# A hybrid decoder step on one core: from one shared front and a 160/384 split to two halves of 256 and 288 columns

## The reference, cut to what matters

```
proj = rmsnorm(x) @ w_in                    # 31 blocks of 128 features (lru, gate, q latent, kv latent, rope key, memory q)
y_lru = rglru(causal_conv(xr)) * gelu(gr)   # a recurrence along the tokens
o_mla = latent attention, 16 heads, causal  # the prompt against itself; the samples also against 2048 cached tokens
o_mem = attention into 256 memory tokens    # the samples against their own cached keys and values
merged = g_l*(y_lru@w_o_lru) + g_a*(o_mla@w_o_mla) + g_m*(o_mem@w_o_mem)
x = x + merged @ w_out
```

```
q = h @ w_peer_query; s = q . sub_keys      # 16 score vectors of 128
top 16 of each, top 16 of the 16x16 sums    # per head: 8 heads x 16 = 128 experts per token
act = gelu(peer_u[idx] . h)                 # 128 rows of 2048 numbers gathered from peer_u
x = x + sum((w * act) * peer_v[idx])        # 128 rows of 2048 numbers gathered from peer_v
y = rmsnorm(x)
```

## Time and profile before

| what | value |
|---|---|
| median of 3 runs | 4582.04 us (4579.02 to 4588.62) |
| span of the profiled execution | 4584.9 us, 2.9 us above the median |
| PE busy | 3686.9 us, 80% |
| DVE busy | 2780.3 us, 61% |
| ACT busy | 391.7 us, 9% |
| POOL busy | 1501.0 us, 33% |
| DMA | 1413.36 MB, mean 308 GB/s |

### The profile page before, as it was taken

One profiled execution on the slowest core, in us unless ns is written; L12 is line 12 of the kernel. 1 busy time (PEld: TensorE's weight loads), 2 busy tenths in 40 slices (PEclk: granted clock), 3 DMA queues, 4 the chain that ended last, 5 costly groups with the idle time before them and its releaser, 6 DMA issues.

```text
span 4584.9 us, 37965 instructions
## 1 busy us (share of the span) xinstructions
PE 3686.9 (80%) x13918; PEld 2304.1 (50%) x13918; DVE 2780.3 (61%) x3641; ACT 391.7 (9%) x882; POOL 1501.0 (33%) x1217
## 2 busy tenths in 40 slices
PE   8999999988999999999999999999999980000000
PEld 6888846653999575555555456444444430000000
DVE  3224324431000167887777568888965569899998
ACT  1012122321000100000000010000000000000000
POOL 0000100024000013454454445444332227777763
PEclk9999999998999999999999999999999995555555
DMA  4121261137666678998999989999999999999998
GB/s 168 65 74 65 101 235 44 42 126 268 239 241 242 231 290 325 395 388 358 422 421 403 375 356 387 404 403 401 394 412 396 423 423 409 398 409 410 411 412 367
DMA packets 223666, 1413.36 MB, mean 308 GB/s; under 512 B 33312, under 2 KB 42400, under 8 KB 59488
## 3 DMA queue, kind: packets, MB, share of 16 engines
q0 software_dynamic: 137424, 904.11, 48.5%
q1 hardware_dynamic: 72768, 471.37, 27.0%
q10 hardware_dynamic: 13296, 35.52, 2.0%
HBM read 1385.11 MB, written 25.75 MB: 308 GB/s over the span
## 4 chain that ended last, share of the span: by engine, by line
PE 71%; DMA 13%; POOL 5%; issue 5%; DVE 4%; ACT 1%; SPq 0%; ACTq 0%; DVEq 0%; POOLq 0%
PE psum L975 26%; PE psum L1116 13%; PE psum L627 12%; DMA arena<-in_v,arena 12%; PE psum L1095 4%; POOL arena L582 3%; DVE psum L2062 3%; POOL arena L602 2%; PE psum L1080 2%; PE psum L1043 1%; PE psum L1023 1%; PE psum L699 1%; PE psum L709 1%; PE psum L869 1%; PE psum L868 1%
## 5 line engine op out<-in xcount | busy, mean ns | idle before, releaser
L975 PE MATMUL psum<-arena 128*128 128x160 f32 (+1 forms) x5120 | 1176.1, 393 | 0.8 <-DVE arena L1746 0.8
L975 PEld LDWEIGHTS psum<-arena 128*128 128x128 f32 x5120 | 836.2, 190 | 340.1 <-DVE arena L1746 0.9
L2062 DVE SCALAR_TENSOR_TENSOR psum<-arena,psum 128x2048 f32<-128x2048 f32 x381 | 897.1, 2355 | 165.1 <-DMA arena<-in_v,arena 155.3
L582 POOL DMA_INDIRECT arena<-in_v,arena x544 | 651.5, 1198 | 742.5 <-DVE psum L2062 325.7
L582 POOL DMA_INDIRECT arena<-in_u,arena x288 | 484.5, 1682 | 1222.2 <-DVE arena L1853 513.4
L1116 PE MATMUL psum<-arena 128*128 128x512 f32 x2048 | 882.2, 594 | 0.6 <-ACT arena L1433 0.6
L1116 PEld LDWEIGHTS psum<-arena 128*128 128x128 f32 x2048 | 390.1, 191 | 492.1 <-issue 492.1
L627 PE MATMUL psum<-arena 128*128 128x272 f32 x2432 | 562.0, 392 | 0.9 <-issue 0.9
L627 PEld LDWEIGHTS psum<-arena 128*128 128x128 f32 x2432 | 460.8, 190 | 98.8 <-issue 5.5
L1940 DVE SCALAR_TENSOR_TENSOR arena<-arena,pages 128x2048 f32<-128x2048 f32 x128 | 300.9, 2351 | 72.6 <-DMA arena<-in_v,arena 67.6
L1897 DVE CUSTOM_DVE_ANT_0 arena<-arena 128x2048 f32<-128x2048 f32 x128 | 287.6, 2288 | 58.7 <-DMA arena<-in_u,arena 57.9
(11 more groups left out here) (298 smaller groups left out, 2675.7 us busy)
## 6 DMA issues: line engine op xcount, KB each, us to landing
arena<-in_w_merge SPq DMA_DIRECT2D x160, 1024.0 KB, 5.6
arena<-in_u_cols SPq DMA_DIRECT2D x128, 1024.0 KB, 9.4
arena<-in_w_out SPq DMA_DIRECT2D x32, 1024.0 KB, 4.9
arena<-in_w_query SPq DMA_DIRECT2D x32, 1024.0 KB, 7.8
arena<-in_w_proj SPq DMA_DIRECT2D x31, 1024.0 KB, 4.8
products<-arena ACTq DMA_DIRECT2D x32, 512.0 KB, 13.8
arena<-in_pool_keys SPq DMA_DIRECT2D x64, 192.0 KB, 4.1
arena<-in_v,arena POOLq DMA_INDIRECT x544, 12.0
```

The source lines that it names most:

```text
L582: pool.indirect_dma_start(row, None, A[table], bass.IndirectOffsetOnAxis(ap=idx[:, r:r + 1], axis=0))\
L975: last = mm(out, w[:, (off + k) * P:(off + k + 1) * P], src[:, k0 + k, lo:hi], start=(k == 0), stop=(k == n - 1))
L2062: V.scalar_tensor_tensor(a, four(row), atmp_b[:, t, r:r + 1], a if r else four(x1_b[:, t, :]), ALU.mult, ALU.add).then_inc(s("rows_used"), 1)
```

## The change

The prompt is cut in two halves, and every stage is run for half A (tiles 0 and 1, 256 columns), then for half B (tiles 2 and 3 and the samples, 288 columns). Memory keys and values are computed once, in A. The projection and latent weights, once streamed for 544 columns, are now streamed twice (31 + 16 DMAs more); the merge, out and query weights were streamed twice already. All weights use one ring of 3 slots (the early stages had 5). The page keys of the samples have 4 slots (5 before).

The rows come in the order `JOBS` = u 0, u 1, v 0, v 1, u 4, v 4, v 2, v 3: tiles 0 and 1 are gathered in full, while half B runs; dense is for tiles 2 and 3. Again 832 rows: 288 u and 544 v. DVE takes them so: 10 during `query_a`, 10 in B's convolutions, 12 in B's recurrence, 8 in B's memory attention, 40 in B's latent attention (80 up to there), none in the attention of the samples, 160 in B's merge, 28 in its out, 4 after it, 40 in its query (312), then 264 beside dense, and 256 in the last loop. The `pairs` of tiles 0 and 1 stand in B's convolutions and recurrence too.

```diff
-A_TILES, B_TILES = (3, 4), (0, 1, 2)
-JOBS = (("u", 3), ("u", 4), ("v", 3), ("v", 4), ("u", 2), ("v", 2), ("v", 0), ("v", 1))
-HELD = 88
+HA = Half("a", 0, HALF, (0, 1), False)
+HB = Half("b", HALF, HALF + SAMP, (2, 3), True)
+JOBS = (("u", 0), ("u", 1), ("v", 0), ("v", 1), ("u", 4), ("v", 4), ("v", 2), ("v", 3))
+FEWER, MORE, MOST = 4, 5, 6
+EARLY_ROWS = 80
...
+STAGES = (("proj_a", NPROJ), ("mem_k", 8), ("mem_v", 8), ("mla_a", 16), ("merge_a", 80), ("out_a", 16), ("query_a", 16),
+          ("proj_b", NPROJ), ("cache", 2 * NB), ("mla_b", 16), ("mla_v", 2), ("merge_b", 80), ("out_b", 16), ("query_b", 16), ("dense", U_TILES))
...
                     c = first_row[table, t] + r
+                    if c == C4:
+                        sample_pages()
...
-                    if (table, t, r) == ("v", 2, HELD):
+                    if (table, t, r) == ("v", 2, MOST - 1):
                         pool.wait_ge(s("products_stored0"), 256)
                         pool.wait_ge(s("products_stored1"), 256)
-                    if table == "v" and t in (2, 0, 1):
-                        if t == 2:
-                            upto = max(0, AHEAD * (r + 1 - HELD) // (n - HELD))
-                        else:
-                            upto = min(AHEAD + P * t + r + 1, DENSE * P)
+                    if table == "v" and t in (2, 3):
+                        upto = min(AHEAD + P * (t - 2) + r + 1, DENSE * P) if t > 2 or r >= MOST - 1 else 0
                         for e in range(asked, upto):
...
+            pe.wait_ge(s("x_normed"), since("x_normed", HB) + KD)
+            projections(HB)
+            memory_attention(HB)
+            latent_attention(HB)
+            sample_attention(HB)
+            merges(HB)
+            output(HB)
+            expert_query(HB)
...
+            for c in range(8):
+                conv(HB, c)
+                if c % 2 == 1 and c < 6:
+                    pairs(0, c + 1)
+                else:
+                    take(2)
+            for c in range(8):
+                if c == 6:
+                    dve.wait_ge(s("proj_stored"), since("proj_stored", HB) + 23)
+                    norm_latents(HB)
+                lru(HB, c)
+                if c < 4:
+                    pairs(1, 2 * c)
+                else:
+                    take(3)
+            turn_krope(HB)
+            memory_attention(HB, take)
+            latent_attention(HB, lambda: take(5))
+            assert taken == EARLY_ROWS, taken
+            sample_attention()
...
+                take(4)
+                if M:
+                    merge_out(HB, M - 1)
+                take(3)
+                products_in(HB, M)
+                take(3)
...
+            chunk_in(0)
+            chunk_out(0)
+            for job, t in enumerate((2, 3)):
+                a = acc[job]
```

More of the change, by code:

```diff
@@ L12 @@
 from contextlib import ExitStack
+from dataclasses import dataclass
 import numpy as np
@@ L34 @@
 T = SEQ + SAMP
-HALF = T // 2
+HALF = 256
 NRNN = 8
@@ new lines, in gates, with square @@
+            def gates(p, M):
+                for j, after in enumerate((1, 2, 4)):
+                    act.wait_ge(w_used, merge_tile(p, M) + after)
+                    if j == 0 and M >= 2:
+                        act.wait_ge(s("merge_step"), since("merge_step", p) + 5 * (M - 1))
+                    a_(gate(p, M, j), gate_bank(p, M, j), ACT.Tanh, scale=0.5).then_inc(s("gate_done"), 1)
+            def square(name, t, out, src):
+                a_(out, src, ACT.Square, accum_out=v("e", t, 1)[0:TILES[t]]).then_inc(s(name + "_squared"), 1)
@@ L1469, in _ @@
+            for k in (5, 6, 7):
+                gelu_chunk(k)
+            act.wait_ge(s("x1_done"), 2)
+            square("fin", 3, four(spare), acc[1])
+            norm_root("fin", 3, 4)
         @block.vector
@@ new lines, in norm @@
+            def norm(name, p, sums, r, nk, nf, x, gain_):
+                dve.wait_ge(s(name + "_summed"), since(name + "_summed", p) + nk)
+                do(V.tensor_scalar(r, sums, 1.0 / nf, EPS, ALU.mult, ALU.add))
+                V.reciprocal(r, r).then_inc(s(name + "_inv"), 1)
+                dve.wait_ge(s(name + "_rms"), since(name + "_rms", p) + 1)
+                for k in range(nk):
+                    V.scalar_tensor_tensor(x(k), x(k), v(gain_, k, 1), r, ALU.mult, ALU.mult).then_inc(s(name + "_normed"), 1)
```

2704 lines of the change are left out of this document (1313 added, 1391 removed).

## The result

The changed kernel takes **4892.26 us** (median, 4883.74 to 4894.34) against 4582.2 of the kernel before on the same chip: a ratio of **1.0676, 95% interval 1.0661 to 1.0691**. Slower, 7 us from the forecast of 4885. The profiled execution took 4890.48 us and its span is 4888.7.

What follows compares the result with a forecast made beforehand. PE was taken to bound the kernel to 1687 us, DMA from there. Last loop's start 4143 + 80 + 650 + 3 + 10 = 4886 on the profile's clock, taken as 4885 us, 6.6% slower; own range 4805 to 4960, chance 0.62.

Steps and rivals of the forecast that it cites:

- The two bounds: Whole kernel before: PE bounds it to 1687 us, from there DMA, which must bring rows and weights.
- Rows beside dense: Dense, 882 us: the byte budget at 402 GB/s allows 194 rows; DVE's list, slowed by ranking, cuts that to 182.
- the rule weighed: DMA ceilings from the Trainium skill: 358 GB/s gives dense 157 rows, end 250 us later; 425 gives 213, 80 earlier.
- Latent attention B: Half B's latent attention: 30.8 us a pair from PE's work, rows at the head and bare waits, 252 in all (203 to 300).
- rival 3: Recurrence and latents B: clock at 1.2 GHz a third of the time, chains 10% longer, some 90 us added, 4975; chance 0.13.
- Samples: The samples' attention: 175 us before, 180 with one key slot fewer, ending at 2142.
- Recurrence B: Half B's recurrence: DVE's steps set it, four of 22.5 us and four of 16.7, plus 9 for latent norms: 166.
- The last loop's start: Start of the last loop: DVE idles 50 us behind POOL's 54 elements; 80 us until rows run at 2.6 each.
- Front of A: Half A from the start, first projection at 28 us, to the end of its query at 1360 us.
- 1 (rows keep pace with dense): Dense: DVE's own list of 907 us is the bound, last loop starts at 3963, end 4706; chance 0.06.
- 2: Halves A and B: waits covered as well as before, merge B starts at 2000 instead of 2142, end 4745; chance 0.16.
- 4 (the shorter last loop decides): Last loop: 256 rows instead of 384 save 333 us if all ahead hides under PE, end 4518; chance 0.03.

Runs made afterwards that it cites:

- e6: Changed kernel with the 256 v rows of tiles 0 and 1 gathered at half their bytes, DVE's work kept: 4852.1 us, ratio 1.0428 to the kernel before.
- e4: Changed kernel with no rows in half B's latent attention, its 40 rows taken later: 4968.3 us, ratio 1.0678 to the kernel before.
- e12: As e9, with three rows instead of two at a pair's end, 88 instead of 80 ahead of merge B: 4827.4 us, ratio 1.0534 to the kernel before.
- e5: The changed kernel, unaltered, on another chip, as the base for other runs: 4947.8 us, ratio 1.0627 to the kernel before.
- e1: Changed kernel with four dummy matmuls ahead of the wait for turned queries in half B's latent attention: 4895.9 us, ratio 1.052 to the kernel before.
- e11: The kernel before with four slots instead of five for the samples' page keys: 4608.1 us, ratio 1.0051 to the kernel before.
- e9: Changed kernel with the edits of e2 and e8 together: 4832.0 us, ratio 1.0538 to the kernel before.
- e7: Changed kernel without the four second ranking steps of tile 1 in B's recurrence, tile 0's experts reused: 4928.0 us, ratio 1.0594 to the kernel before.
- e3: Changed kernel with 48 of the 54 elements gathered one behind each of the last 48 rows ahead of the last loop: 4944.5 us, ratio 1.0628.
- e8: Changed kernel with 32 elements instead of 54 in one piece in the last loop, then two behind each row: 4937.9 us, ratio 1.0613.
- e2: Changed kernel with two of the five rows per pair in B's latent attention moved to the pair's end: 4875.0 us, ratio 1.0471.
- e10: As e9, with more dummy matmuls in the samples' attention, ahead of the third key page and the turning: 4840.0 us, ratio 1.0556.

## Why the forecast came out, and where its steps did not

**The two bounds: right.** DMA is half idle or more for most of the time until merge B, and decides from there. Merge B took 623 us (forecast 633: the 8 us for bytes were not needed, DMA gave 410 GB/s where 404 were asked), dense 882 (882) at 405 GB/s, the last loop 678 from its first row (691). e6 shows that DMA holds the rows, e4 and e12 are in line with 2.6 us for a row behind merge B.

**Rows beside dense: 195, not 182.** The byte budget had said 194. What failed was the deduction for DVE's list: it is nearly full while it ranks (175 of 200 us, e5), and fewer bytes come then (386 GB/s against 426 behind it), but the 402 GB/s of the budget are a mean over such stretches of the kernel before, so the deduction counted the ranking twice. Of the rule weighed, neither ceiling set the time: it had 157 rows by the lower and 213 by the upper, and dense brought 195 at 405 GB/s. The 13 rows would be worth 34 us by the forecast's own 2.6; measured was 19 (205 forecast from dense to the last loop, 186 measured). The rest went to two small terms that were too low: DVE waits for nearly every row around 3974, so the "five of them loaded" did not lie ready, and at the samples' first u row it waits 7.75 us where the whole handover had been put at 5.

**Latent attention B: the miss, 298 us instead of 252.** "30.8 a pair" was right for its mechanism (e1: 31.4), but the wait of 3.85 us that it contains let the clock fall to 1.2 GHz for the scores and some matmuls behind them, 8.8 us more a pair (40.25 against 31.4). That was rival 3's mechanism, at one of its places, and I had given it 0.13. The forecast named the wait and did not ask what follows it. In A, with short waits only, a pair takes 16.8 (17.3).

**Samples: 185 instead of 180, by a wrong term.** The key slot costs 26 us (e11) instead of 5; 175 + 26 would be 201, and 200 is what the stage takes in e9, where it begins at 1916 instead of 1998; so the 185 hangs on how late it began. Which transfers had been asked for by then I have not traced.

**Recurrence B: right in sum, not in its working.** 4 x 22.5 + 4 x 16.7 were to be DVE's steps. DVE's steps took 21.25 and 15.4, but PE ran six of its steps at its own 16.5 us without a wait, and then waited 12.0, 13.6 and 7.4 us. Without the pairs only the first wait goes (e7). So DVE's 13 us of pairs a step do not pace the stage; PE's 100 us and the chain of the last steps behind it (1556 to 1608 in e7) do.

**The last loop's start: right.** 47.35 us of wait forecast as 50, then DVE waits again six rows later (DMA brings 16 GB/s from 4211 to 4240). But the one piece of elements was not the cheap thing to mend that it looked: e3 moved it and got nothing, e8 6 us at most.

**Front of A: 18 us faster than forecast** by 1342 us, from the start (22 instead of 28), the memory attention, the output and the query. With +41 at merge B (in which the front's 18 are counted), -5 in merge, out and query B, -19 behind dense, -1 at the start of the last loop and -13 in it the errors add to +3. That the end came within 7 us is luck: the forecast is nearer than its steps are.

**Rivals.** 1 (rows keep pace with dense) fell: the last loop starts at 4211, not 3963. 2 fell: merge B at 2183, not 2000. 4 (the shorter last loop decides) fell: it would have had to start before 3840. With the mend of e2 and e8 the change is still 5.4% slower than the kernel before; the best found, e9 and e12, beat the changed kernel and not the one before. What remains is what the forecast called the detour: merge B at 2115 (e9) instead of 1687, of which some 280 us are what A's own merge, output and query take over those of the smaller part before (809 us against 528), while of 832 rows only 80 are brought ahead of it.

## What to carry to other kernels

Read a reordering as two budgets, PE's list up to the point from which bytes decide, and bytes from there; work put at the front of PE's list costs its full time if DMA has nothing to bring meanwhile. Where a term of the forecast holds an idle time of PE of some microseconds, read the granted clock behind the nearest such idle time in the trace and price it: here the clock cost three times what the wait did, and splitting two rows off the head of a pair took both away. Measure a wait before it is filled: dummies that are longer than the wait hold up what stands behind them (the first pair of e1, e10). And where POOL issues gathers beside DVE, count its issues per DVE row, not POOL's busy time alone (e3).

## What the runs showed of the hardware

POOL's issue of a gather takes 0.94 us with DVE idle and 0.97 beside DVE instructions with one large operand in SBUF. Begun while DVE is in an instruction that reads two, it ends 0.80 to 0.82 us behind that instruction's end (283 of 288 in the changed kernel), 1.94 to 2.08 us in the mean; it hides under DMA's 2.6 us for a row, and comes to light as soon as anything else is issued with it. An idle PE of 3.85 us was followed by 19 us of full work at 1.2 GHz (granted clock 0.50 from 1775.00 to 1793.90, 1.00 from 1794.30), and so were, nearly alike, the waits of 3.70 to 4.14 us in the other six of the seven pairs; waits of 2.81 us in some pairs and not in others (e12), waits of 0.60 or 0.77 in none. Dummy matmuls of 0.9 us each in the wait kept the clock. Rows of 4 KB filled DMA (share 0.97) at 353 GB/s, rows of 8 KB (1.01) at 426. Four chips gave 4582, 4586, 4654 and 4656 us for one kernel, and two of them 1.0676 and 1.0627 for the same change.
